# First norm of a two-layer hybrid encoder: shift and scale taken from raw weights on TensorE, by channel tile

## The reference, cut to what matters

```
c_act = silu(c)                                     # c: 1 x 1024
mod   = c_act @ ada_w[l] + ada_b[l]                 # ada_w[l]: 1024 x 6144
sh1, sc1, g1, sh2, sc2, g2 = split(mod, 6)
h     = rmsnorm(x, norm1_g[l]) * (1 + sc1) + sh1    # x: 1024 positions x 1024 channels
proj  = h @ w_in                                    # q, k, v and 16 forget gates
y     = forgetting_attention(...)
x     = x + g1 * y
```

## Time and profile before

| | |
|---|---|
| median of 3 executions | 2566.41 us (2560.12 to 2568.66) |
| the profiled execution | 2563.79 us, of which 2562.0 us are the span of the core |
| first matmul of the value projection | 54.46 us |
| first reader of its result (L1666) | 80.42 us |
| busy: TensorE 2371.5 us | 93% of the span |
| busy: VectorE 1583.9, ScalarE 1150.2, GpSimd 1133.5 us | 62%, 45%, 44% |
| DMA | 205.41 MB, mean 80 GB/s |

### The profile page before, as it was taken

The page is one execution under the profiler, slowest core; times in us unless marked ns, Lnnn a source line. Parts: engine busy times, 40 slices in busy tenths (PEclk is TensorE's granted clock), DMA queues, the critical chain, the costliest instruction groups (busy, mean ns, idle before and its releaser), DMA issues.

```text
span 2562.0 us, 31418 instructions
## 1 busy us (share of the span) xinstructions
PE 2371.5 (93%) x11208; PEld 1968.7 (77%) x11208; DVE 1583.9 (62%) x2579; ACT 1150.2 (45%) x1933; POOL 1133.5 (44%) x1568
## 2 busy tenths in 40 slices
PE   5999999898998999999999988987989999999996
PEld 3878788786777878888888877776777888888884
DVE  5575765757428677777775676774285455554446
ACT  4365564646416333333333375663164334333344
POOL 1411312121144666666666443113446666666660
PEclk8999999998899999999999998987999999999998
DMA  6121222223310333433331122114101111112111
GB/s 246 59 91 54 83 83 63 76 65 99 123 46 28 97 116 119 119 119 117 118 121 58 58 99 64 50 42 173 42 28 55 58 50 50 50 50 64 52 58 66
DMA packets 98731, 205.41 MB, mean 80 GB/s; under 512 B 9856, under 2 KB 59648, under 8 KB 98448
## 3 DMA queue, kind: packets, MB, share of 16 engines
q1 hardware_dynamic: 31808, 109.06, 13.5%
q10 hardware_dynamic: 66768, 94.35, 11.7%
HBM read 185.09 MB, written 16.32 MB: 79 GB/s over the span
## 4 chain that ended last, share of the span: by engine, by line
PE 68%; DVE 16%; ACT 7%; DMA 4%; issue 4%; POOL 1%; ACTq 1%; DVEq 0%; SPq 0%; POOLq 0%
PE bank L882 41%; PE bank L614 16%; DVE ada_acc_f L1622 1%; DVE bank L1700 1%; DVE X L1891 1%; PE bank L810 1%; PE bank L749 1%; PE bank L664 1%; DVE PL L1726 1%; PE bank L775 1%; PE bank L785 1%; PE bank L1064 1%; PE bank L811 1%; PE bank L812 1%; DVE ada_acc L1622 1%
## 5 line engine op out<-in xcount | busy, mean ns | idle before, releaser
L882 PE MATMUL bank<-H,w_spl 128*128 128x512 f32 x3744 | 879.4, 393 | 25.3 <-DVE H L1606 14.6
L882 PEld LDWEIGHTS bank<-H,w_spl 128*128 128x128 f32 x3744 | 704.1, 189 | 182.3 <-issue 16.2
L543 POOL TENSOR_TENSOR w_spl<-w_raw,w_spl 128x256 fp32r<-128x256 f32 x688 | 529.3, 796 | 458.5 <-ACT w_spl L1360 457.0
L614 PE MATMUL bank<-H,w_spl 128*128 128x512 f32 x2016 | 506.1, 401 | 25.2 <-DVE H L1606 11.9
L882 PE MATMUL bank<-TB,w_spl 128*128 128x512 f32 x2112 | 494.8, 390 | 0.4 <-ACT sU L1375 0.4
L614 PEld LDWEIGHTS bank<-H,w_spl 128*128 128x128 f32 x2016 | 379.0, 192 | 107.2 <-issue 18.8
L882 PEld LDWEIGHTS bank<-TB,w_spl 128*128 128x128 f32 x2112 | 395.0, 188 | 83.2 <-issue 1.2
L1360 ACT ACTIVATE w_spl<-w_raw 128x512 fp32r<-128x512 f32 x328 | 201.8, 628 | 530.8 <-PE bank L882 369.4
L486 POOL TENSOR_TENSOR pace<-one_s 128x1 f32<-128x1 f32 x50 | 13.3, 267 | 806.7 <-PE bank L775 377.1
L1891 DVE SCALAR_TENSOR_TENSOR X<-bank,mods,X 128x1024 f32<-128x1024 f32 x176 | 225.0, 1278 | 34.4 <-PE bank L882 34.3
L1884 DVE TENSOR_TENSOR bank<-bank,sU 128x512 f32<-128x512 f32 x80 | 55.9, 699 | 269.4 <-PE bank L882 269.3
(11 more groups left out here) (179 smaller groups left out, 3310.4 us busy)
## 6 DMA issues: line engine op xcount, KB each, us to landing
w_raw<-in_w_stream SPq DMA_DIRECT2D x184, 512.0 KB, 3.7
ada_raw_f<-in_ada_w ACTq DMA_DIRECT2D x192, 128.0 KB, 2.3
ada_raw_a<-in_ada_w ACTq DMA_DIRECT2D x32, 512.0 KB, 3.9
ada_raw<-in_ada_w SPq DMA_DIRECT2D x8, 1024.0 KB, 14.4
negF<-scratch_f ACTq DMA_DIRECT2D x16, 512.0 KB, 3.8
ada_raw_f<-in_kv_ada_w ACTq DMA_DIRECT2D x64, 128.0 KB, 2.5
X<-in_x_t SPq DMA_DIRECT2D x4, 1024.0 KB, 10.8
X<-in_x_t ACTq DMA_DIRECT2D x4, 1024.0 KB, 8.0
```

The costliest lines, as they stand in the source:

```text
L543: last = pool.tensor_tensor(block_at(layer, b, 1, q, q + 256), src[:, q:q + 256], block_at(layer, b, 0, q, q + 256).bitcast(F32), ALU.subt ...
L614: last = pe.matmul(dst, stat(k, a), mov(k, b), start=(k == 0 and a + b == 0), stop=(k == KT - 1 and a == 1))
L882: last = pe.matmul(dst, block_at(layer, b, x, k * P, k * P + P), mov(y), start=(start and x + y == 0), stop=(stop and x == 1), skip_group_ ...
```

## The change

The columns of `ada_w[0]` are laid out on the host by channel tile: `ada_first[kt]` holds, for one tile of 128 channels, the 128 columns of the shift and the 128 of the scale over all 1024 rows (1 MB, 8 KB a partition). The eight pieces go into the memory that `H` takes later, one per channel tile. TensorE multiplies the raw weights by `c_act` itself: for each channel tile 2 x 8 matmuls (shift and scale, eight row tiles, added up in PSUM) with a stationary operand of 128x128 float32 and one moving column. VectorE adds the bias and makes the factor for that tile alone. SP's queue has the input first, then the two tiles of value weights, then the eight pieces, then the third tile. The sum of squares is made as in the later norms. On TensorE, four channel tiles of shift and scale come ahead of the value projection and the other four lie between its channel tiles; the eighth tile of positions is computed at the end, since its bank 7 takes the results of shift and scale until then.

```diff
-        ada_raw0 = at("ada_raw0", [P, 4, KT, 512], F32, 0)
+        ada_raw0 = at("ada_raw0", [P, KT, 2, KT, P], F32, 0)
...
-            load(0, 0, None)
-            load(1, 1, None)
             for j in range(4):
                 sp.dma_start(X[:, 2 * j:2 * j + 2], x_t.rearrange("k p s -> p k s")[
                     :, 2 * j:2 * j + 2]).then_inc(x_in[j], 16)
+            load(0, 0, None)
+            load(1, 1, None)
+            for kt in range(KT):
+                sp.dma_start(ada_raw0[:, kt].rearrange("p a k n -> p (a k n)"), ada_first[kt]).then_inc(ada0_in[kt], 16)
             load(2, 2, 1)
-            for j in range(4):
-                for half in range(2):
-                    sp.dma_start(ada_raw0[:, j, 4 * half:4 * half + 4], ada_w[0].rearrange("(k p) n -> p k n", p=P)[
-                        :, 4 * half:4 * half + 4, 512 * j:512 * j + 512]).then_inc(ada0_in[2 * j + half], 16)
...
             def square_sum(n, release=0, released=w_used):
-                pe.wait_ge(ss_done, 7 * n)
+                pe.wait_ge(ss_done, 7 * n + 7)
...
-            for k in range(KT):
-                pe.wait_ge(sq_done, k + 1)
-                over_partitions(sq[:, k % 2], k == 0, k == KT - 1)
-            for j in range(4):
-                ada_cols(ada_acc0[:, j], 4, 8 * (j + 1), 2 + j, 0, ada0_step)
-
+            square_sum(0)
+
+            def ada_first_cols(kt):
+
+                pe.wait_ge(ada0_in[kt], 16)
+                if kt == 0:
+                    pe.wait_ge(cact_done, 1)
+                else:
+
+                    pe.wait_ge(ada_ev, kt)
+                for i in range(2):
+                    for k in range(KT):
+                        last = pe.matmul(bank(7, 2 * kt + i, 2 * kt + i + 1), ada_raw0[:, kt, i, k], c_act[:, k:k + 1],
+                                         start=(k == 0), stop=(k == KT - 1))
+                last.then_inc(ada_ps, 1)
+
+            def v_first(k, tt):
+                for a, b in ((0, 0), (0, 1), (1, 0)):
+                    last = pe.matmul(bank(tt, 0, 272), H[:, k, a, tt * P:tt * P + P], wvg[:, k, b, :],
+                                     start=(k == 0 and a + b == 0), stop=(k == KT - 1 and a == 1))
+                    if k + tt + a + b == 0:
+
+                        last.then_inc(w_used, 2)
+                if k == KT - 1:
+                    last.then_inc(v_ps, 1)
+
+            for kt in range(4):
+                ada_first_cols(kt)
             pe.wait_ge(w_ready, 2)
             pe.wait_ge(vg_in, 1)
             for k in range(KT):
                 pe.wait_ge(h_lo, k + 1)
...
+                for tt in range(7):
+                    v_first(k, tt)
+                if k < 4:
+                    ada_first_cols(k + 4)
+
+            pe.wait_ge(ada_ev, KT)
+            for k in range(KT):
+                v_first(k, 7)
...
-            for j in range(4):
-                for half in range(2):
-                    dve.wait_ge(ada0_in[2 * j + half], 16)
-                    ada_steps(ada_acc0[:, j], lambda k: ada_raw0[:, j, k, :], 8 * j, ks=range(4 * half, 4 * half + 4),
-                              steps=ada0_step)
...
+            for j in range(7):
+                add_squares(0)(j)
...
+            def first_mods(kt):
+
+                dve.wait_ge(ada_ps, kt + 1)
+                V_.tensor_tensor(mods[:, kt:kt + 9:8], bank(7, 2 * kt, 2 * kt + 2), modb[:, kt:kt + 9:8],
                                  ALU.add).then_inc(ada_ev, 1)
...
+                dve.wait_ge(ada_ev, kt + 1)
+                V_.scalar_tensor_tensor(coef[:, kt:kt + 1], mods[:, M_SC1 + kt:M_SC1 + kt + 1], 1.0,
+                                        gain[:, G_N1 + kt:G_N1 + kt + 1], ALU.add, ALU.mult)
...
+            for k in range(KT + 1):
+                if k < KT:
+                    first_mods(k)
+                    if k == 0:
+                        dve.wait_ge(rs_done, 1)
+                    scaled(0, k, h_hi)
+                if k == 0:
+                    dve.wait_ge(const_r, 1)
+                    V_.tensor_tensor(wvg[:, :, 1, 256:272], wf_raw[:], wvg[:, :, 0, 256:272].bitcast(F32),
+                                     ALU.subtract).then_inc(vg_in, 1)
+                if k:
+                    low(0, k - 1)
```

More of the change, by code:

```diff
@@ L168, in qk_done, with program @@
     return [n for n, k in (qk_steps(g, T - 1) if T else []) if k == KT - 1]
-def program(nc, x_t, c_t, ada_w, kv_ada_w, mod_b, gains, w_stream, w_f, b_f, sinks, conv, ident, mask,
+def program(nc, x_t, c_t, ada_first, ada_w, kv_ada_w, mod_b, gains, w_stream, w_f, b_f, sinks, conv, ident, mask,
             stair, alibi, out_t):
@@ L313, in program @@
         ada_in = sem("ada_in")
-        ada0_step = sem("ada0_step")
         ada_step = sem("ada_step")
@@ L400, in program @@
         y_out = [sem(f"y_out{i}") for i in range(2)]
-        N_ADA_A = 4 + 4 * NG
+        ADA_0 = KT
+        N_ADA_A = ADA_0 + 4 * NG
         ADA_STEPS_A = 8 * 4 * NG
@@ L815, in _ @@
             for c in range(NM):
-                maximum(0, c, 4)
+                maximum(0, c, ADA_0)
                 if c < 4:
@@ L829, in _ @@
                     for c in maxima_at(MAX_V, tt):
-                        maximum(4 * g, c, 4 + 4 * g)
+                        maximum(4 * g, c, ADA_0 + 4 * g)
                     if tt == 6:
@@ L839, in _ @@
                         for c in maxima_at(MAX_T[hl], t):
-                            maximum(4 * g + hl + 1, c, 4 + 4 * g + hl)
+                            maximum(4 * g + hl + 1, c, ADA_0 + 4 * g + hl)
                     if hl < 3 and t == 10:
@@ L1103, in one @@
                     if k >= 2:
-                        act.wait_ge(ss_done if n else sum_ps, 7 * (n - 1) + k - 1 if n else k - 1)
+                        act.wait_ge(ss_done, 7 * n + k - 1)
                     nc.scalar.activation(sq[:, k % 2], X[:, k], ACT.Square).then_inc(sq_done, 1)
@@ L1110, in root @@
                 nc.scalar.preload_act_table_set("natural_log_exp_and_others")
-                act.wait_ge(sum_ps, 8 + 2 * n)
+                act.wait_ge(sum_ps, 2 * n + 2)
                 nc.scalar.activation(dst[:], pair(0), ACT.Ln, bias=eps_s[:], scale=1.0 / D).then_inc(rt_done, 1)
@@ L1586, in one @@
                     else:
-                        dve.wait_ge(ss_done, 7 * (n - 1) + k)
+                        dve.wait_ge(ss_done, 7 * n + k)
                         V_.tensor_tensor(ss[:], ss[:], sq[:, k % 2], ALU.add).then_inc(ss_done, 1)
@@ L1628, in _ @@
             V_.memset(ones[:], 1.0).then_inc(set_done, 1)
[L1629 to L1633, removed]
[L1634 to L1652 removed]
+            for j in range(7):
+                add_squares(0)(j)
+            dve.wait_ge(id_done, 1)
+            def first_mods(kt):
+                dve.wait_ge(ada_ps, kt + 1)
+                V_.tensor_tensor(mods[:, kt:kt + 9:8], bank(7, 2 * kt, 2 * kt + 2), modb[:, kt:kt + 9:8],
+                                 ALU.add).then_inc(ada_ev, 1)
+                dve.wait_ge(ada_ev, kt + 1)
[13 more added lines that the diff above has]
+                    low(0, k - 1)
             V_.tensor_tensor(sel[0:16, :], id_f[0:16, 0:8], id_f[0:16, 8:16], ALU.add)
@@ L1749, in ada_mods @@
             def ada_mods(piece):
-                dve.wait_ge(ada_ps, 4 + piece + 1)
+                dve.wait_ge(ada_ps, ADA_0 + piece + 1)
                 V_.tensor_tensor(mods[:, 16 + 2 * piece:18 + 2 * piece], bank(1, 0, 2),
@@ L2055, in _ @@
                 scaled(5, k, y_done)
-INPUTS = ["x_t", "c_t", "ada_w", "kv_ada_w", "mod_b", "gains", "w_stream", "w_f", "b_f", "sinks", "conv",
+INPUTS = ["x_t", "c_t", "ada_first", "ada_w", "kv_ada_w", "mod_b", "gains", "w_stream", "w_f", "b_f", "sinks", "conv",
           "ident", "mask", "stair", "alibi"]
@@ L2114, in layout @@
         "kv_ada_w": a["kv_ada_w"],
+        "ada_first": a["ada_w"][0][:, 0:2 * D].reshape(KT, P, 2, KT, P).transpose(3, 1, 2, 0, 4).reshape(KT, P, 2 * D),
         "mod_b": np.concatenate([cols(a["ada_b"][0]), cols(a["ada_b"][1]), cols(a["kv_ada_b"])], axis=1),
```

1 line of the change is left out of this document (removed).

## The result

| | before | changed |
|---|---|---|
| median | 2567.42 us (4 runs) | 2599.41 us (2595.69 to 2603.83, 4 runs) |
| ratio, 95% interval | | 1.0132 [1.0117, 1.0147] |
| profiled execution | 2563.79 us | 2603.83 us |
| reader of the value projection | 80.42 us | 116.14 us |

The change costs 32 us. The mark, VectorE's first read of the value projection, moved by 35.7 us; the distance from there to the end was 2481.6 us before and is 2485.9 us here. In the other kernels of this study that distance lies between 2474 and 2489 us, so nothing behind the mark can be told from no change. The mark shows where in the opening the time goes, but it is read from one execution of each kernel, and here that is the slowest of the four, 4.4 us above the median. A difference of marks is therefore given together with the difference of medians wherever the two disagree.

A forecast was written before the change was run, and what follows sets the result against it. VectorE's accumulation, ending last, was taken to set the value projection's start. Sum of squares, groups, alternating stretch, value parts and position tile moved the mark from 80.4 to 111.1 us (+30.7), giving 2596 us; range 2574 to 2609.

The forecast's parts named there:

- the sum of squares: Opening, additions on VectorE and eight TensorE records: done at 31.4 us against 32.0 before, so nothing won.
- groups 0 to 3: First four sets of 32 one-column pairs, ahead of the value projection: from 31.4 to 58.5 us.
- the alternating stretch: Four times a value part and a group on TensorE: 38 us, between 25.8 all fast and 48.6 all slow.
- the last value parts: Four value parts alone, 10.1 us plus 1.6 for a slow start, then the eighth position tile, 2.9: to 111.1.
- The product on TensorE: Shift and scale as 256 record pairs: 7.0 us per group of 32 at 1.2 GHz, 3.6 at 2.4.
- Group 0: First 32 one-column pairs, behind the sum of squares: 5.0 us, the clock falling in it, to 36.4.
- the earlier trace: Sliding-window attention before the change: TensorE busy 2.00 of 2.00 us, clock at 0.50; taken as sign of slow groups.
- A: Rival: clock stays at 2.4 GHz through the groups; mark at 86.0 us, +5.6 us, 2569; chance 0.08.
- B: Rival: everything slow until value parts stand alone; mark 121.7 us, 2605 to 2608; edge of own case, 0.85 together.
- C: Rival: pairs much cheaper in a long run, deciding from 0.09 us down; at 0.06, 2556 us; chance 0.04.
- D: Rival: the opening stretch is cheaper than it looks or hidden later; no change, 2566 us; chance 0.03.
- The rule weighed: Skill's clock rule, read as busy time: groups stay at 2.4 GHz, sum +5 us instead of +31; prediction went against it.

The follow-up runs named there:

- e1: Changed kernel with 128 equal moving columns instead of one in each of the 128 new matmuls; 2580.1 us, 1.0056 of the kernel before.
- e5: Changed kernel with the edits of e1 and e2 together; 2571.3 us, 1.0023 of the kernel before.
- e7: Changed kernel with tiles 0, 1, 4, 5 on TensorE (128 equal columns), the others accumulated on VectorE, value weights first; 2556.1 us, 0.9960 of the kernel before.
- e8: e7 with one moving column instead of 128 equal ones; 2564.3 us, 0.9991 of the kernel before.
- e3: Changed kernel with the sum of squares made on TensorE tile by tile again, no additions on VectorE; 2598.2 us, 1.0122 of the kernel before.
- e2: Changed kernel with the two tiles of value weights loaded ahead of the input again; 2594.5 us, 1.0113 of the kernel before.
- e6: Changed kernel with all eight one-column groups ahead of the value projection, none between its channel tiles; 2602.7 us, 1.0145 of the kernel before.

## Why the prediction was right

**The direction and the size.** Slower was given 0.87; the median, 2599.4 us, lies 3.4 us above the 2596 forecast and inside the range. The mark was forecast at 111.1 us and came at 116.1, in an execution 4.4 us slower than the median. By terms the 5.0 us are 5.8 for the sum of squares, less 1.2 for groups 0 to 3 and 0.8 for the alternating stretch, and 1.2 more for the last value parts.

**The product on TensorE, the deciding term.** 7.0 us a group at 1.2 GHz: groups 1 to 3 took 6.97. The 0.35 us between groups was 0.33 (48.55 to 48.88 us). Group 0 at 5.0: it took 3.95, as the clock fell only near 40 us. That the clock stays low although TensorE is busy was taken from the earlier trace rows, and it came true.

**Where the reason was weaker than the result.** The matmuls of the earlier trace rows have 128 columns, and their clock stays at 0.50 from 1720 to 1734 us, with TensorE busy for 13.8 of the 14 us. By that comparison e1's pairs, which also move 128 columns beside the same kind of load, should have stayed at 0.50; they ran at 1.00 throughout, and so did those of e5 and, from 36 us on, of e7. So the earlier trace rows showed that busy time alone does not give the high clock, but not that width makes the difference. That one column against 128 makes it for these pairs is shown by e1 and, in another order of work, by e7 against e8. The stretch of the earlier trace rows begins behind 2.6 us without a matmul, with the clock already down; but so does the first group of e7, and it speeds up on its way (12 records in the 2 us from 22 us, 15 in the 2 us from 24 us). Why the matmuls of the earlier trace rows stay low is open, and in this step the prediction was right with some luck.

**The middle value for the alternating stretch.** 38 us were taken between 25.8 and 48.6, a little above their midpoint of 37.2; it took 63.1 to 100.3, 37.2 us. The picture behind it held too: a value part at the low clock of 4.8 us, a group behind it either fast (3.84, 3.65, 4.48) or slow (6.62). The size was a midpoint and not derived, so this closeness is luck; in the profiled execution of e3 the same stretch took 34.4 us.

**The last value parts.** 84 and 24 matmuls at 11.7 + 2.9 = 14.6 us; measured 15.8.

**The term that was mis-sized: the sum of squares.** The prediction had it done at 31.4 us, from a start of the additions at 16.4 us, additions of 1.67 us at worst and 5.4 us on TensorE. It was done at 37.2. Three things add up. The start was 17.95 us (1.5 late), since with the input first the small constant landed 1.2 us later, where I had called that wait unchanged, and since the copy ahead of the additions took 1.13 us and not 0.69 (e2). The additions beside GpSimd's subtraction took 3.2 us and not 1.67, where the row that bounded them lay beside instructions of GpSimd with 256 elements, and the splits here have 1,024; they ended at 30.4 and not 26. And TensorE took 6.7 us and not 5.4, all eight records at the length that they have at the low clock; this part differs between executions of the same code, with 5.1 us in e1 and 6.4 in e6. In all 5.8 us, more than the whole gap of 5.0 at the mark.

**The rivals.** A, the clock stays high: the windows of the changed kernel exclude it, and e1 shows what it would have given, though only with more columns. From the first group to the mark A had 54.6 us (31.4 to 86.0); e1 took 54.7 (35.36 to 90.09) and e5 as much (29.51 to 84.23). B, everything slow: groups 4, 6 and 7 were not, so the alternating stretch took 37.2 of B's 48.6 us; the mark came only 5.6 us under B's, because the sum of squares, which B had as early as my own case, was late. C, pairs far cheaper in a long run: a full-clock group took 3.63 us (e3), 0.11 us a pair, above the 0.09 at which it would have decided. D: the distance from the mark to the end did not shrink.

**The rule weighed.** The sentence of the Trainium skill (TensorE: Matmul & The Clock Gate, "What's actually happening") that the clock follows how busy the engine has been would, read as busy time, have put the mark at 86 us, 30 below the measured one; read so, the trace does not agree with it (0.50 with matmuls in 22.9 of the 24 us from 40 to 64). The load's price of 107 ns in its section "LDWEIGHTS (loading the stationary operand)" is near what a pair took at the full clock (3.63/32 = 0.113 us in e3) and half of what one took at the low clock (6.97/32 = 0.218 us).

## What to carry to other kernels

A product with a vector on TensorE cost here a weight load for each 128x128 tile, nearly the same whether one column or 128 were moved (3.63 and 3.73 us a group at the same clock), and almost twice as much at the low clock (6.97). With one column the clock did not stay high, so it was worth moving 128 equal columns. Work taken off an engine that is only a few microseconds late pays only as far as its new place is free; here a division between both engines, with the wide operand, beat either. After a change in the order of loads, look at what else starts when its data now lands: GpSimd's splits came to lie on VectorE's additions, which cost 4.6 us, and a small constant came later, which cost most of another 1.6.

## What was not expected of the hardware

- Columns that carry nothing new are cheap: moving 128 equal columns instead of one in 128 matmuls made the kernel 19 us faster (2599.4 to 2580.1), and the group of 32 pairs took 3.73 us (e1) against 3.63 with one column at the same clock (e3), both directly behind the sum of squares.
- Two overlapping instructions of VectorE and GpSimd can both be stretched: 1.22 to 3.2 us and 2.34 to 3.20 us.
- The pieces of 8 KB a partition came in at 418 to 424 GB/s in the windows from 20 to 36 us, the same bytes in rows of 2 KB at 386 to 389 GB/s in the kernel before. Nothing in the changed kernel waited for it, and neither the row size nor the order of the pieces was tried by itself, so the cause is not shown.
- The granted clock's column reads 1.00 from the start of the span, while the first square sum's records were as long as at 1.2 GHz (6.71 us for eight, 3.43 in e7). In this stretch the text goes by the lengths of the records and not by the column.
- Which groups between value parts ran fast differed from kernel to kernel: one slow of four in the changed kernel and in e2, none in e3's profiled execution. In another place the same question is open: 128 columns ran at 1.00 in e1 and at 0.50 in the earlier trace rows. What decides it was not settled; e3's spread of 18 us over four executions suggests that it also differs between executions of one kernel, and that was not traced.
